# A decoder trunk step on one core: two G blocks computed as a tenth pair of half products, and the small branch work around them reordered

## The reference, cut to what matters

```python
h = rmsnorm(x, lp['norm_mix'])
z = h @ lp['w_in']
qa, ka, va, qb, fb, ib, gb, xc, gc, xd, gl = jnp.split(z, split_at, axis=-1)
...
o_b, S_new = hgrn2(qb, fb, ib, gb, S0, lp)       # linear recurrence, times silu(gb)
o_c, h_new, conv_c_new = rg_lru(xc, gc, ...)     # conv of xc, two small gates, scan, times gelu(gc)
o_d, pool_new = pool_mixer(xd, ...)              # trailing means, small projection
...
gates = jax.nn.sigmoid(gl.reshape(B, L, N_BRANCH, D_MODEL))
x = x + jnp.sum(gates * proj, axis=2) @ lp['w_out']
```

## Time and profile before

| | us |
|---|---|
| median of three runs | 1760.36 |
| lowest and highest | 1759.42, 1762.21 |
| the profiled execution | 1758.6 |
| its span in the trace | 1756.8 |
| PE busy | 1730.7 (99%) |
| DVE / ACT / POOL busy | 1117.1 / 731.0 / 778.8 |

### The profile page before, as it was taken

The page is one execution under the profiler, slowest core; times in us unless marked ns, Lnnn a source line. Parts: engine busy times, 40 slices in busy tenths (PEclk is TensorE's granted clock), DMA queues, the critical chain, the costliest instruction groups (busy, mean ns, idle before and its releaser), DMA issues.

```text
span 1756.8 us, 30899 instructions
## 1 busy us (share of the span) xinstructions
PE 1730.7 (99%) x12865; PEld 1679.8 (96%) x12865; DVE 1117.1 (64%) x1255; ACT 731.0 (42%) x1034; POOL 778.8 (44%) x531
## 2 busy tenths in 40 slices
PE   8999999999999999999999999999999999999998
PEld 8999999998999878899999999999999999999998
DVE  6931114656765177657744877888888887675744
ACT  6433332463421456612235544445444442333521
POOL 1666673431122212212133476667776636667021
PEclk9999999999999999999999999999999999999999
DMA  6543225132122532547523223233222375334032
GB/s 228 76 126 115 98 74 202 49 97 79 66 82 67 195 106 74 168 172 257 195 87 134 99 74 111 105 110 110 98 98 98 114 288 208 116 117 148 26 126 96
DMA packets 84655, 214.80 MB, mean 122 GB/s; under 512 B 14851, under 2 KB 31779, under 8 KB 83363
## 3 DMA queue, kind: packets, MB, share of 16 engines
q1 hardware_dynamic: 73570, 189.48, 31.6%
q0 software_dynamic: 4032, 14.68, 2.7%
q10 hardware_dynamic: 6912, 8.65, 1.4%
HBM read 149.48 MB, written 63.40 MB: 121 GB/s over the span
## 4 chain that ended last, share of the span: by engine, by line
PE 92%; DVE 3%; ACT 2%; DMA 1%; issue 1%; POOL 0%; SPq 0%; ACTq 0%; DVEq 0%; POOLq 0%
PE ps L1636 24%; PE ps L1086 21%; PE ps L1073 11%; PE ps L1684 10%; PE ps L1216 10%; PE ps L1668 3%; PE ps L1304 2%; PE ps L1171 1%; PE ps L1060 1%; PE ps L1389 1%; PE ps L1113 1%; DMA masks<-in_wb 1%; PE ps L1553 1%; PE ps L1423 1%; PE ps L1410 1%
## 5 line engine op out<-in xcount | busy, mean ns | idle before, releaser
L3318 POOL TENSOR_TENSOR Wl<-BIG,Wh 128x512 fp32r<-128x512 f32 x110 | 142.8, 1308 | 118.0 <-ACT Wh L2185 117.9
L3175 POOL CAST Uh<-BIG 128x1024 fp32r<-128x1024 f32 x27 | 35.8, 1326 | 286.6 <-PE ps L1073 199.4
L2969 DVE SCALAR_TENSOR_TENSOR ps<-BIG,fpar,ps 128x1023 f32<-128x1023 f32 x84 | 107.9, 1285 | 35.9 <-ACT ps L2276 35.0
L1073 PE MATMUL ps<-Hh,Uh 128*128 128x352 f32 x384 | 128.3, 334 | 0.8 <-ACT BIG L1926 0.8
L2539 DVE TENSOR_TENSOR BIG<-BIG,ps 128x528 f32<-128x528 f32 x45 | 31.7, 704 | 148.1 <-PE ps L1216 147.8
L1073 PE MATMUL ps<-Hh,Ul 128*128 128x352 f32 x384 | 123.6, 322 | 0.0
L1073 PE MATMUL ps<-Hl,Uh 128*128 128x352 f32 x384 | 123.3, 321 | 0.0
L3270 POOL TENSOR_TENSOR Ul<-BIG,Uh 128x1024 fp32r<-128x1024 f32 x15 | 36.1, 2412 | 164.6 <-ACT Uh L2145 164.6
L1636 PE MATMUL ps<-Hl,Wh 128*128 128x264 f32 x528 | 107.2, 284 | 0.0
L2958 DVE TENSOR_TENSOR BIG<-BIG,ps 128x528 f32<-128x528 f32 x110 | 77.3, 703 | 43.1 <-PE ps L1636 37.3
L1684 PE MATMUL ps<-Sl,Vh 128*128 128x264 f32 x504 | 102.0, 284 | 0.0
(11 more groups left out here) (467 smaller groups left out, 5574.6 us busy)
## 6 DMA issues: line engine op xcount, KB each, us to landing
BIG<-in_wu SPq DMA_DIRECT2D x44, 512.0 KB, 4.6
hidden<-BIG SPq DMA_DIRECT2D x22, 528.0 KB, 2.7
late_gates<-BIG SPq DMA_DIRECT2D x18, 528.0 KB, 3.0
BIG<-sums SPq DMA_DIRECT2D x12, 792.0 KB, 4.8
BIG<-in_wgl SPq DMA_DIRECT2D x9, 1024.0 KB, 5.9
BIG<-in_wd SPq DMA_DIRECT2D x6, 1536.0 KB, 10.4
H<-late_gates SPq DMA_DIRECT2D x17, 528.0 KB, 3.7
gates<-BIG ACTq DMA_DIRECT2D x48, 176.0 KB, 2.0
```

The costliest lines, as they stand in the source:

```text
L1073: ins = nc.tensor.matmul(psb(fill_bank(p)), w[:, u % 2, k], x[:, k, part * PART:part * PART + PART], start=(k == 0 and w is Uh and x is Hh ...
L2969: link(v.scalar_tensor_tensor(y[:, back:SEQ], x[:, 0:SEQ - back], w, y[:, back:SEQ], ALU.mult, ALU.add), v.scalar_tensor_tensor(ys[:, :, b ...
L3318: nc.gpsimd.tensor_tensor(Wl[:, b], src, Wh[:, b].bitcast(F32), ALU.subtract).then_inc(S("w_lo"), 1)
```

## The change

The two G tiles are no longer z blocks. Their weights stand last in wz (Z_COLS), are loaded as pair 1 of now ten pairs (Z_PAIR), and their rows go through GY to late_gates without the sigmoid. After the last pair SP loads them back into Z[GB]. The small weights wrg and wpool change places, so that those of C0 are there early. PE's order after the pairs becomes C00, C01, QB0, QB1, C10, C11, FB0, first I row, FB1 (with the third group of the first row behind its first step), second I row, D0, D1, VA0, VA1. On DVE the first convolution is cut in two around the third sum of the last pair, and the first scan stretch moves ahead of the means. On ACT `rates`, `decay`, `root` and `gelu` of a half come ahead of the Q tiles (first half) and of the F tiles (second half).

```diff
-ZB = 14
+ZB = 12
...
+Z_PAIR = 1
+PAIRS = (4 * LATE - COVER) // 2 + 1
```

SP, after the last pair:

```diff
+            for half in range(2):
+                sp.wait_ge(*upto(f"g_stored{half}", 16 * (Z_PAIR + 1)))
+            sp.dma_start(Z[:, GB:GB + 2, :], late_gates[2 * Z_PAIR:2 * Z_PAIR + 2].rearrange("i p t -> p i t"))\
+                .then_inc(S("cd_in"), 16)
+            sp.dma_start(wrg[1], a["wrg"][:, 1]).then_inc(S("cd_in"), 16)
+            sp.dma_start(wpool, a["wpool"]).then_inc(S("cd_in"), 16)
             gate_out(PAIRS - 1, 0)
             gate_out(PAIRS - 1, 1)
```

PE, after the last pair:

```diff
+            pe.wait_ge(S("cd_in"), 80)
+            unit("C00", wrg[0][:, 0], cX[:, 0], 1)
             pe.wait_ge(*upto("g_sum", 5 * PAIRS - 1))
+            unit("C01", wrg[0][:, 1], cX[:, 0], 1)
+            for i in range(2):
+                block_z(f"QB{i}")
+            pe.wait_ge(S("cd_in"), 144)
             for g in range(2):
+                unit(f"C1{g}", wrg[1][:, g], cX[:, 1], 2)
+            block_z("FB0")
+            pe.wait_ge(S("pool_read"), 2)
+            turned_v(0, turn[:, 0], range(2))
+            block_z("FB1", (0, lambda: turned_v(0, turn[:, 0], (2,))))
+            turned_v(1, turn[:, 1], range(2))
+            unit("D0", wpool[:, 0], Z[:, XD], 3)
+            turned_v(1, turn[:, 1], (2,))
+            unit("D1", wpool[:, 1], Z[:, XD + 1], 4)
```

ACT:

```diff
             for i in range(2):
+                rates(i)
+                decay(i)
+                root(i)
+                gelu(i)
+                for g in range(2):
+                    z_out(("QB", "FB")[i] + str(g), (QB, FB)[i][:, g])
+                    if i:
+                        act.wait_ge(S("pool_read"), 2)
+                        turned_v(g)
```

DVE (`scanned(i)` is the scan stretch of one half, unchanged in itself; `scanned(1)` stays behind the means):

```diff
                     if c == PAIRS - 1 and part == T1:
                         dve.wait_ge(S("cd_in"), 80)
                         dve.wait_ge(*upto("gw_first", 32))
-                        convolved(0)
+                        convolved(0, (3, 2))
+                    elif c == PAIRS - 1 and part == T4:
+                        convolved(0, (1, 0))
                     gate_sum(c, part)
-            convolved(1)
+            convolved(1, (3, 2, 1, 0))
+            scanned(0)
```

More of the change, by code:

```diff
@@ L236 @@
 assert sum(n for _, n in PLACES) == 3 * FILLS
-USERS = ("XC0", "XC1", "XD0", "XD1", "GC0", "GC1", "IB0", "IB1", "QB0", "QB1", "C00", "C01", "FB0", "FB1", "D0", "D1",
-         "C10", "C11", "GB0", "GB1", "VA0", "VA1")
-RING = ("XD0", "XD1", "GC0", "GC1", "IB0", "IB1", "QB0", "QB1", "FB0", "FB1", "GB0", "GB1", "VA0", "VA1")
+USERS = ("XC0", "XC1", "XD0", "XD1", "GC0", "GC1", "IB0", "IB1", "C00", "C01", "QB0", "QB1", "C10", "C11", "FB0", "FB1",
+         "D0", "D1", "VA0", "VA1")
+RING = ("XD0", "XD1", "GC0", "GC1", "IB0", "IB1", "QB0", "QB1", "FB0", "FB1", "VA0", "VA1")
 FRONT = RING.index("IB1") + 1
@@ L1850, in gate_sig @@
                     act.wait_ge(*upto("g_copied", 2 * c + 2))
[L1851 removed]
+                if c == Z_PAIR:
+                    act.sem_inc(on("g_sig"), 1)
+                else:
+                    nc.scalar.activation(GY[:, half], GY[:, half], ACT.Sigmoid).then_inc(on("g_sig"), 1)
             act.wait_ge(S("zc_done"), 2)
@@ L1935, in before @@
                 act.wait_ge(S("d_rows"), 16)
-                for user in ("FB0", "QB0", "GB0"):
+                for user in ("FB0", "QB0"):
                     z_wait(user)
-                for user in ("FB1", "QB1", "GB1"):
+                for user in ("FB1", "QB1"):
                     z_wait(user)
+                act.wait_ge(S("cd_in"), 144)
                 link(nc.scalar.activation(bE, f, ACT.Abs))
@@ L2556, in _ @@
+                if taps[-1] == 0:
+                    dve.sem_inc(S("cd_ready"), 1)
             for c in range(PAIRS):
```

125 lines of the change are left out of this document (49 added, 76 removed).

## The result

| | before | changed |
|---|---|---|
| median of nine runs, us | 1760.47 | 1766.02 |
| lowest and highest | 1759.42, 1762.21 | 1762.36, 1770.82 |
| ratio, with 95% interval | | 1.0034 [1.0024, 1.0044] |
| profiled execution, us | 1758.6 | 1766.02 |
| span in the trace | 1756.8 | 1764.2 |

The change makes the kernel 0.34% slower. The forecast said 1762.1, no difference that can be measured, and a range up to 1766.0; the median lies 0.02 us above that. The nine runs of the changed kernel also lie three times as far apart as the nine of the kernel before (8.5 us against 2.8; 35 more runs of the kernel before lie 5.2 us apart), and that turned out to be the better clue.

A forecast was written before the change was run, and what follows sets the result against it. PE, busy 99% of the span, bounds the kernel. Gains of 7.1 us (2.7 + 4.4) are eaten by 0.6 + 0.4 + 4.7 + 1.3, V rows add 1.8: execution 1760.3, median 1.8 above, 1762.1; range 1756.0 to 1766.0.

The forecast's parts named there:

- 15.8 (18.7 minus 2.9 POOL blocking): ACT's before(), first step to VA0's read: 18.7 us, less 2.9 of DVE steps behind POOL that now fall elsewhere.
- Behind the V rows nothing changes: After the turned V rows: no further gain or loss; branch B's next chain keeps over 1 us of reserve.
- the third case: D rows' store ends late: at 10 us PE waits 4.9 ahead of the V rows, clock costs 1.3; 1766.4; chance 0.23.
- G as a pair: Pairs and z blocks: a tenth pair of 20.6 us replaces two z blocks of 23.3, so −2.7 us.
- The last pair: At B22: PE's 3.2 us wait shrinks to 0.3 and the clock stays up, so −4.4 us.
- C0 ahead of Q: After the pairs: QB0 waits 0.6 us; QB1 waits nothing, at most 0.4, for its weight.
- DVE and ACT: First step of FB1: DVE's chain makes ACT's first copy late, PE waits 4.2 to 5.2 us, FB1 ends at 353.2.
- I let FB1 also pay 1.3: FB1: low clock behind its wait costs 1.3 of the 1.5 us that B22 paid.
- The half microsecond between the two orders of issue: First step of FB1: middle of 341.6 taken for ACT's copy; DVE ahead of POOL's cast gives 341.1, sum 0.5 lower.
- D behind the turned rows: FB1 to V rows: D store 7.0 us, before() 15.8; turned V rows wait 1.8 us more.
- the third rival: D rows' store ends late, at 10 us instead of 7.0, deciding from about 8.3; 1766.4; chance 0.23.
- a second drop of the clock at the V rows: Listed sign of being wrong: PE's clock falls again at the turned V rows.

The follow-up runs named there:

- tap_only: Kernel before with only the first convolution's four taps split in two pairs around the third sum of the last pair; 1755.20 us, ratio 0.9975.
- look 1: The changed kernel as it is, run again for a second trace; 1772.11 us.
- lock_off: Changed kernel with GpSimd's subtraction of the weight split after VA1's held back until VectorE's last step of before() that ScalarE needs; 1764.89 us, ratio 1.0030.
- d_early: Changed kernel with ScalarE's first F tile and turned row ahead of root and gelu, and D0, D1 between FB0 and FB1; 1755.17 us, ratio 0.9970.
- wb_late: Kernel before with the mixing stage's third next wb load issued later, behind the next wait for a sum; 1761.8 us, ratio 1.0005.

## Why the prediction failed

Two steps failed, and a third was priced at nothing where it counted. "15.8 (18.7 minus 2.9 POOL blocking)": `before()` took 19.7 us. "Behind the V rows nothing changes": the mixing stage took 4.5 us more. And the low clock behind the V rows stood in the third case only.

**G as a pair**: right. From the start of the pairs to the third product of the last one the trace has 194.11 us, before 173.53: 20.58 us for the tenth pair, for a forecast of 20.59.

```profile
106.11 194.09 PE ps L1227 x1584
300.22 4.88 DMA BIG<-early_rows
```

**The last pair**: right. B22 waits 0.3 us and takes 3.17; tap_only gave 4.3 us for a forecast of 4.4.

**C0 ahead of Q**: QB0 waits 0.4 for 0.6, QB1 doesn't wait.

**DVE and ACT**: right in its mechanism, too high in its price. VectorE's scan stretch ran from 322.15 to 335.1 and the means to 354.2, where the steps had given 335.9 and 355.1; the first copy was there at 360.6 for 362.2. PE waited 2.7 us for 4.7. "I let FB1 also pay 1.3" did not come true in this trace, where the clock stayed up and FB1 ended at 371.1 instead of 373.8. It was no bad guess: in four of the seven traces with this wait the clock fell and FB1 paid 1.1 to 1.5. What decides it isn't shown, and it isn't the wait's length (2.7 us in three of the four, 3.0 in look 1, where it did not fall). The half microsecond between the two orders of issue was real: VectorE went first, and GpSimd's cast took 1.97 us instead of 1.03, which is how the Trainium skill's rule in "SBUF — State Buffer", "Who interferes with whom", would have it.

**D behind the turned rows**: here two terms were wrong, with opposite signs. The store of the D rows took 5.7 us, not 7.0, although the store of the C rows was issued 0.4 us behind it, and 5.4 to 5.9 in the other traces of this order; so the third rival was as good as out. (The prediction says that the two gate stores fit completion out of order. They don't show it: issued 1 us apart, they took 7.8 and 8.0 us and so landed in the order of issue.) But "15.8 (18.7 minus 2.9 POOL blocking)" took away a price without asking where it would go. `before()` took 19.7 us, because GpSimd's subtraction now met its first step (3.45 us for 1.26) and its cast a later one (1.02 us for 0.18). lock_off measured 16.6 without that. The wait ahead of the V rows was 4.4 us. I had named "a second drop of the clock at the V rows" among the signs of being wrong, and it is what happened; but I priced it in the third case only, at 1.3 us, where in the traces it cost up to 6 us more in one execution than in another.

**"Behind the V rows nothing changes"**: the sentence that cost most in the profiled execution. I had looked at the next chain of branch B and its reserve of over 1 us, not at the rest of the kernel. Some 370 us later one load had landed just in time, with 0.3 us of wait behind it. In the changed kernel it came 1.0 to 1.8 us later after its issue, and that cost 1.0 to 4.6 us, the high values where the clock fell too. Why it lands later there is not settled: it isn't the rows' place in DRAM, the same bytes stand ahead of it, and it isn't the wait ahead of the V rows either. It took 11.3 to 12.2 us in all eight traces with the G pair and the load in its old place, d_early among them, and 10.4 to 10.7 in the three such traces of the old order.

**The sum**: 1760.3 was forecast for the profiled execution. FB1 ended 2.7 us earlier than forecast, the stretch from there to the end of the turned V rows took 3.5 more, and what lies behind 4.9 more, 4.5 of it in the mixing stage; that is the 1766.0 measured. The median came out at the same value, so the difference of 1.8 us between execution and median, taken over from the kernel before, was wrong as well. With five of nine runs above the range, two of them by 0.02 us, the chance of 0.55 for no difference was too high and that of 0.30 for slower too low.

## What to carry over

A stall that has been taken out of one path (an interference of two engines, a wait) has to be laid down again in the new order, not subtracted. A wait of a few microseconds on TensorE is to be priced with the low clock behind it, and as a range: in the dense block FB1 the clock was low for 0 or 3.4 us behind a wait of 2.7 to 3.0, behind the turned V rows, where the work is sparse, for 3.4 to 20.5 us behind 4.4. That the sparse work makes the difference is my reading, not shown. One trace doesn't show this: the first of the changed kernel has no fall of the clock in FB1, and four of the six others of the same order have one. And an unchanged stage far behind a change isn't safe if one of its loads lands with less reserve than the shift may move it; look for waits of a few tenths there before writing that nothing changes.

## What the runs showed of the hardware

The same program (the changed kernel), with the same wait of 4.4 us ahead of the same work, ran at half clock for 3.4, 13.6 and 20.5 us in three executions. Behind a wait put in alone, doubling it from 3.3 to 6.5 us added 3.7 us and no spread. With waits of 0.8 us at most in the same place the clock fell in two of eight traces: d_early (low from about 400 to 407 us) and wb_late (409 to 412), not in the kernel before. And behind a wait of 2.7 to 3.0 us in FB1 it fell in four of seven.

Eight small steps of VectorE (32 partitions by 128) took 7.85 us beside two GpSimd subtractions and a cast (lock_off), 4.48 beside one subtraction (the changed kernel) and 2.45 without (the kernel before): together they lose about as long as GpSimd's work beside them lasts (5.4 us for 5.8, 2.0 for 2.3), so small steps are no protection.
